# All eight later modulation blocks summed on VectorE, their columns by products with ones, and a new order of attention and routing

## The chip, the cores and the metric

The kernel runs on one core of one Trainium2 chip, in float32 throughout. The metric is the device time of one execution, in microseconds (us). Time before: 1838.23 us, the median of 3 runs (1836.99 to 1841.49).

## What is computed

Two layers of a hybrid diffusion backbone work on 128 prompt tokens and 256 sample tokens of width 1024 (three tiles of 128 tokens). Each layer has two halves:

```
mod = silu(c) @ w_mod + b_mod        # one row for the prompt, one for the sample, 6 x 1024
sh1, sc1, g1, sh2, sc2, g2 = split(mod, 6)
h = rmsnorm(x) * (1 + sc1) + sh1
x = x + g1 * token_mixing(h)         # pooling, windowed attention, latent attention; three gates; one output projection
h = rmsnorm(x) * (1 + sc2) + sh2
x = x + g2 * experts(h)              # router softmax; each of 16 experts takes its best tokens (16 prompt, 32 sample)
```

In blocks of 512 columns the modulation has twelve blocks, and 0 to 3 are sh1 and sc1, 4 and 5 g1, 6 and 7 sh2, 8 and 9 sc2, 10 and 11 g2. sh2 and sc2 are needed as columns (feature on the partition) for the router and the expert input; g1 and g2 as rows.

## The kernel before

**Weights.** SyncE's queue (SP) brings the mixing weights as 57 units of up to 1 MB (`plan_units`, issued in the order `ISSUE`) into a ring of 8 slots. Unit n is issued only when unit n - 8 has been used (`wait_mixing`), and the queue waits in order. The expert weights come as 96 double units of 2 MB a layer (12 for each pair of experts) into 8 double slots; the first three are issued behind the unit `AFTER_ATTENTION`, the others of the first eight when their slots are free, and each further one when the double unit before it in its slot has been used (`load_group`).

**Two ways to a block.** `mod` (line 1509) makes a block on TensorE: 8 products of 32 columns of the conditioning with 512 columns of weights, four of them side by side in the array; ScalarE copies the row out (`mod_row`) and `mod_cols` (line 1521) turns it into columns by four products with the two-column constant `pair`, which VectorE's `mod_cols` (1031) reads. Blocks 0 to 3 and 6 to 9 go this way. `sum_rows` (line 1268) makes a block on VectorE: for each of 8 parts of the weights and each of the two streams one scalar_tensor_tensor adds weights times conditioning to a row that starts as the bias (copied in by POOL's queue); one product with ones then adds over the partitions. Blocks 4, 5, 10 and 11 (`SUMMED`) go this way.

**Order of a layer** (TensorE, from line 1640): blocks 0 to 3 and the turned input; the segments of the input projection; u for the pooling (line 1666); block 6; the turned queries `tq` (1677), keys `tkc` (1682, 1685) and latents `tkv` (1692); block 7; the query projection `wq` (1704); the pooled products (1710); blocks 8 and 9; the key and value projection `wkv` for four tiles (1731), with the turned query heads `tqm` and key heads `tkm` (1725) in between, and the columns of blocks 6 to 9 (`modcol` 1, line 1739) between the second and third key tile. VectorE normalises heads there (`query`, `key`, with POOL's power). Then eight steps m of attention, a pair of heads each: gate product (1565), values of the step before (1605, 1608), branch product (1584), turned probabilities (1593), second gate, turned probabilities, scores of the next step (1550 to 1556), second branch. Gates and branches all use bank 7; ScalarE reads a gate (tanh, 769), VectorE reads a branch (`merge`, 1070). VectorE finds the maxima (`maxima`, 1083 to 1092), ScalarE the exponentials (755 to 762), VectorE divides (`divide`, 1105) and sums blocks 4 and 5 at the end of a step. Then the third gate and branch (8 steps), with blocks 10 and 11 summed.

**Output and routing** (from line 1878). `project_out(n, t, lo, hi)` (1795) makes half n of tile t; VectorE adds it to x (`add_mixed`, 1321 and 1325). Tiles go in the order 1, 2, 0 (the sample is 1 and 2). For each: `turn_x`, ScalarE's `square_x`, `router` (1819), `route` (1827), softmax (`logits`, `affinities`), then for the sample and for the prompt `turn_affinities` (1834), `top` (rounds of MAX8 and MATCH_REPLACE8), `number`, `turn_slots`, `chosen`, and `gather_sample` (1862) and `gather_prompt` (1873), which pick the tokens of four experts out of the scaled x (`normal_x`) by products. `gathered` scales them with sh2 and sc2 on ScalarE (952, 954) and VectorE (1432, 1434) and gives them to the expert products (`project`, 1925). `gate_row` (1849) makes rows of g2, which ScalarE copies out (940).

```
for n, i in enumerate(SUMMED):
    if n >= 2:
        wait_full(pool, l, ("modb", SUMMED[n - 2], 1))
...
if c == 0:
    pe.wait_ge(xcur_ready, (l * NG + gr + 1) * 12)
    for b in range(4):
        begin_pair(b, 1)
```

Of the kernel before, what the change touches and what calls it, by code (L numbers as in the profile page):

```python
# [8 lines left out]
ALU = mybir.AluOpType  # L9
# [97 lines left out]
MODROW = {0: 0, 2: 1, 1: 0, 3: 1, 6: 0, 7: 1}  # L107
# [6 lines left out]
def plan_banks(l):  # L114
# [19 lines left out]
    use(("mod", 6), 1)  # L134
# [6 lines left out]
    use(("mod", 7), 7)  # L141
# [5 lines left out]
    for i in (8, 9):  # L147
        use(("mod", i), (7, 0)[i % 2])
# [6 lines left out]
    for t in range(4):  # L155
        if t == 2:
            use(("modcol", 1), 3)
        for h in range(2):
            use(("tkm", t, h), (3 + 2 * t + h) % 8 if t < 3 else 1 + h)
    for m in range(NM):  # L160
        for j in range(2):
            use(("sa", m, j), 2 * j)
            use(("sb", m, j), 2 * j + 1)
        for j in range(2):
            use(("x", m, j), 4)
            use(("y", m, j), 5)
        use(("o", m), 6)
        for j in (2 * m, 2 * m + 1):
            use(("gate", j // 8, j % 8), 7)
            use(("br", j // 8, j % 8), 7)  # L170
    for i in (4, 5):
# [6 lines left out]
    for name, b in ((("wo", 0, 1), 5), (("wo", 1, 1), 6), (("wo", 0, 2), 7), (("xt", 1, 0), 0), (("xt", 1, 1), 1),  # L178
                    (("wo", 1, 2), 5), (("rpart", 1), 2), (("wo", 0, 0), 6), (("xt", 2, 0), 0), (("xt", 2, 1), 1),
                    (("route", 1), 3), (("rpart", 2), 2), (("wo", 1, 0), 7), (("route", 2), 3), (("xt", 0, 0), 5),  # L180
                    (("afft", 0), 4), (("modb", 10, 0), 6), (("xt", 0, 1), 5), (("modb", 11, 0), 7), (("rpart", 0), 4),
                    (("route", 0), 6), (("slt", 0), 5), (("afft", 1), 6), (("slt", 1), 7)):
# [21 lines left out]
def plan_units():  # L204
# [5 lines left out]
    for i in (6, 7):  # L210
        units += [("mod", i, 0), ("mod", i, 1)]
    units += [("wq", 0, 0), ("wq", 1, 0)]
    for i in (8, 9):
        units += [("mod", i, 0), ("mod", i, 1)]
    units += [("wkv", 0, 0)]
    for b in range(3):
        for h in range(2):
            if b < 2:
                units += [("mod", 4 + b, h)]
            units += [("gate", (b, h), 0), ("gate", (b, h), 1), ("br", (b, h), 0)]  # L220
    for i in (10, 11):
        units += [("mod", i, 0), ("mod", i, 1)]
    for n in range(2):
        units += [("wo", n, 0), ("wo", n, 1)]
# [17 lines left out]
SUMMED = (4, 5, 10, 11)  # L242
# [22 lines left out]
def hybrid_step(nc, a, outs):  # L265
    with ExitStack() as ctx:
# [76 lines left out]
        wsh = view(12800, 2, KB, NE)  # L343
# [50 lines left out]
        bias_in = [sem(f"bias_in{i}") for i in SUMMED]  # L394
# [1685 lines left out]
```

## Time and profile before

| what | value |
|---|---|
| median of 3 runs | 1838.23 us |
| profiled execution, its own time | 1838.3 us |
| its span, first to last instruction | 1836.3 us |
| mean granted TensorE clock | 0.992 of 2.4 GHz |
| TensorE matmuls busy | 1719.0 us, 94% |
| VectorE, ScalarE, GpSimd busy | 568.3, 295.3, 117.4 us |
| HBM traffic over the span | 290 GB/s |

One execution was recorded. Times of rows are us from the first instruction; PE is TensorE, PEld its weight loads, DVE VectorE, ACT ScalarE, POOL GpSimd, SP SyncE; a q behind the name is the engine's own queue. L1565 is line 1565. A float32 product leaves two matmul records. Layer 0 runs to about 925 us, layer 1 follows.

### The profile page before, as it was taken

What the parts mean: (1) busy time and instruction counts of PE and PEld (TensorE: products, weight loads), DVE (VectorE), ACT (ScalarE), POOL (GpSimd) and SP (SyncE); (2) the same over time, 40 slices, a digit from 0 to 9 for tenths busy, and PEclk for the clock granted to TensorE, in tenths of its full rate; (3) what the DMA queues carried; (4) which work ended last, traced back from release to release, by engine and by line L of the source; (5) the groups of instructions that cost most, each with busy time, mean ns of one, the idle gap of its engine ahead of it and who ended that gap; (6) DMA issues with size and microseconds to landing.
All of it is one profiled execution on the core that took longest, in us unless ns stands there. A gap on an engine that the chain in (4) does not pass through costs nothing.

```text
span 1836.3 us, 18935 instructions
## 1 busy us (share of the span) xinstructions
PE 1719.0 (94%) x7216; PEld 803.3 (44%) x7216; DVE 568.3 (31%) x1245; ACT 295.3 (16%) x741; POOL 117.4 (6%) x160
## 2 busy tenths in 40 slices
PE   6998999999899988898899999999999999988987
PEld 3555555554434332242245555555544342323322
DVE  1345544352322111121124355442541221201211
ACT  2234222200200010000022333221021010100100
POOL 1151000000000000000012410000000000000000
PEclk9999999999999999999999999999999999999999
DMA  9453222354799999999993712225547999999997
GB/s 379 186 205 136 85 99 92 142 205 180 284 430 430 431 431 431 431 430 431 428 366 118 281 46 92 92 92 240 206 155 308 430 430 432 430 431 430 430 430 322
DMA packets 49104, 533.79 MB, mean 291 GB/s; under 512 B 5840, under 2 KB 6896, under 8 KB 10384
## 3 DMA queue, kind: packets, MB, share of 16 engines
q1 hardware_dynamic: 45776, 524.39, 68.3%
q0 software_dynamic: 2112, 7.97, 1.1%
q8 instruction: 43, 0.70, 0.1%
q10 hardware_dynamic: 1152, 0.56, 0.1%
q14 instruction: 21, 0.17, 0.0%
HBM read 530.76 MB, written 2.13 MB: 290 GB/s over the span
## 4 chain that ended last, share of the span: by engine, by line
PE 74%; DMA 21%; DVE 2%; ACT 1%; issue 1%; SPq 0%; ACTq 0%; POOL 0%; DVEq 0%; POOLq 0%
PE bank L1925 21%; DMA ring<-in_w_moe 20%; PE bank L1565 13%; PE bank L1584 7%; PE bank L1630 6%; PE bank L1962 5%; PE bank L1795 5%; PE bank L1666 2%; PE bank L1862 2%; PE bank L1731 2%; PE bank L1515 1%; PE bank L1593 1%; PE bank L1704 1%; PE bank L1608 1%; PE bank L1553 1%; PE bank L1556 1%
## 5 line engine op out<-in xcount | busy, mean ns | idle before, releaser
L1565 PE MATMUL bank<-hT,ring 128*128 128x384 f32 x768 | 259.0, 491 | 8.2 <-DVE xn L1070 4.3
L1925 PE MATMUL bank<-M,hT 128*64 128x512 f32 x1024 | 228.8, 595 | 23.6 <-DMA M<-in_w_moe 19.8
L1925 PE MATMUL bank<-ring,hT 128*64 128x512 f32 x1024 | 227.2, 595 | 11.3 <-DMA ring<-in_w_moe 11.3
L1565 PEld LDWEIGHTS bank<-hT,ring 128*128 128x128 f32 x768 | 143.2, 190 | 113.6 <-DVE xn L1070 7.9
L1925 PEld LDWEIGHTS bank<-M,hT 128*64 128x64 f32 x1024 | 72.7, 137 | 170.3 <-issue 139.3
L1925 PEld LDWEIGHTS bank<-ring,hT 128*64 128x64 f32 x1024 | 72.5, 137 | 157.9 <-issue 139.5
L1584 PE MATMUL bank<-M,ring 128*128 128x384 f32 x384 | 134.2, 492 | 4.8 <-ACT M L769 4.8
L1925 PE MATMUL bank<-ring,M 128*64 128x512 f32 x512 | 115.4, 596 | 18.6 <-DMA ring<-in_w_moe 18.6
L1925 PE MATMUL bank<-M 128*64 128x512 f32 x512 | 115.6, 595 | 12.3 <-DMA M<-in_w_moe 12.3
L1630 PE MATMUL bank<-ring,hT 128*128 128x512 f32 (+1 forms) x288 | 119.3, 574 | 1.7 <-DVE hT L1062 1.7
L962 ACT ACTIVATE hT<-bank 128x512 f32<-128x512 f32 x32 | 19.1, 597 | 574.2 <-PE bank L1925 574.2
L1584 PEld LDWEIGHTS bank<-M,ring 128*128 128x128 f32 x384 | 71.0, 190 | 59.8 <-issue 7.9
L1962 PE MATMUL bank<-M 128*128 128x512 f32 x192 | 93.7, 621 | 3.3 <-DVE M L1457 3.3
L1444 DVE SCALAR_TENSOR_TENSOR hT<-hT,bank 128x512 f32<-128x512 f32 x32 | 22.0, 688 | 233.9 <-ACT hT L962 233.9
L1449 DVE SCALAR_TENSOR_TENSOR hT<-hT,bank 128x512 f32<-128x512 f32 x32 | 22.0, 688 | 213.1 <-PE bank L1925 213.1
L1457 DVE TENSOR_TENSOR M<-bank,g2slot 128x512 f32<-128x512 f32 x32 | 22.1, 691 | 210.7 <-PE bank L1925 210.7
L1795 PE MATMUL bank<-ring,xn 128*128 128x512 f32 x192 | 85.4, 596 | 0.0
L1630 PEld LDWEIGHTS bank<-ring,hT 128*128 128x128 f32 x288 | 55.0, 193 | 63.7 <-issue 63.7
L608 POOL TENSOR_TENSOR rstd<-var,mhalf 128x8 f32<-128x8 f32 (+2 forms) x38 | 47.2, 1244 | 470.6 <-DVE var L986 470.5
L1925 PEld LDWEIGHTS bank<-ring,M 128*64 128x64 f32 x512 | 36.9, 137 | 90.3 <-issue 77.8
L1468 DVE TENSOR_TENSOR x<-x,bank 128x512 f32<-128x512 f32 x96 | 66.0, 688 | 30.1 <-PE bank L1962 30.1
L1925 PEld LDWEIGHTS bank<-M 128*64 128x64 f32 x512 | 37.3, 137 | 83.2 <-issue 79.1
(229 smaller groups left out, 1547.4 us busy)
## 6 DMA issues: line engine op xcount, KB each, us to landing
M<-in_w_moe SPq DMA_DIRECT2D x96, 2048.0 KB, 31.6
ring<-in_w_moe SPq DMA_DIRECT2D x96, 2048.0 KB, 30.6
ring<-in_w_mix SPq DMA_DIRECT2D x110, 1024.0 KB, 8.6
ring<-in_w_mix SPq DMA_DIRECT2D x4, 576.0 KB, 4.7
modrow<-in_bias_rows POOLq DMA_DIRECT2D x4, 512.0 KB, 6.7
g2slot<-in_bias_rows POOLq DMA_DIRECT2D x4, 512.0 KB, 7.6
M<-in_counts POOLq DMA_DIRECT2D x2, 768.0 KB, 12.3
out<-x SPq DMA_DIRECT2D x6, 256.0 KB, 2.0
```

What stands on the lines that cost most here:

```text
L608: nc.gpsimd.tensor_tensor(rstd[:, c0:c0 + n], var[:, c0:c0 + n], mhalf[:, 0:n], ALU.pow)\
L1457: V.tensor_tensor(osb[:, n * 512:(n + 1) * 512], bank[b][:, :], g2slot[:, n * 512:(n + 1) * 512], ALU.mult).then_inc(bank_read[b], 1)
L1468: V.tensor_tensor(xs, xs, bank[b][:, :], ALU.add).then_inc(bank_read[b], 1)
L1565: ins = mm(ps[:, 0:TOK], w[:, q, (j % 4) * P:(j % 4 + 1) * P], hT[:, 4 * h + q, :], start=(h == 0 and q == 0), stop=(h == 1 and q == 3))
L1584: ins = mm(ps[:, 0:TOK], w[:, q, (j % 4) * P:(j % 4 + 1) * P], y[:, q, :], start=(q == 0), stop=(q == 3))
L1630: ins = mm(ps[:, 0:n], hT[:, 4 * h + q, t * P:(t + 1) * P], w[:, q, 0:n], start=(h == 0 and q == 0), stop=(h == 1 and q == 3))
L1666: ins = mm(ps[:, 0:TOK], w[:, q, g * P:(g + 1) * P], hT[:, 4 * h + q, :], start=(h == 0 and q == 0), stop=(h == 1 and q == 3))
L1731: ins = mm(ps[:, :], ckvT[:, k, t * P:(t + 1) * P], w[:, k, h * 512:(h + 1) * 512], start=(k == 0), stop=(k == 1))
L1795: ins = mm(ps[:, :], merged[:, kb, t * P:(t + 1) * P], w[:, kb % 4, :], start=(kb == 0), stop=(kb == 7))
L1862: mm(v[:, :, CP:USED], xn[:, t, kb * P:(kb + 1) * P], gsel[:, t, :].rearrange("p (e s) -> p e s", s=SLOTS)[:, :, CP:USED], start=(t == 1), ...
L1925: ins = mm(bank[b][64 * e:64 * e + 64, :], lhs(e, 4 * h + q), w[:, q, :], start=(h == 0 and q == 0), stop=(h == 1 and q == 3))
L1962: mm(bank[b][:, :], selT[:, t * P:(t + 1) * P], osb[:, n * 512:(n + 1) * 512], start=True, stop=True).then_inc(bank_full[b], 1)
```

## The change

The eight blocks 6 to 9, 4, 5, 10 and 11 are now all summed on VectorE. Blocks 6 to 9 are summed in the eight steps of attention without a bias row (the first product is a tensor_scalar; the bias comes in with the columns), half a unit at a time; 4, 5 and 10 in the stage of the third gate; 11 among the additions of the output projection. Their columns are made by `column`: eight products with one column of ones each. The order of units, of banks, of the copies of turned tiles, of attention, of output projection and of routing changes, and the expert products wait for the two halves of their input apart. The core of the diff:

```diff
@@ plan_units
-    for i in (6, 7):
-        units += [("mod", i, 0), ("mod", i, 1)]
-    units += [("wq", 0, 0), ("wq", 1, 0)]
-    for i in (8, 9):
-        units += [("mod", i, 0), ("mod", i, 1)]
-    units += [("wkv", 0, 0)]
...
+    units += [("wq", 0, 0), ("wq", 1, 0), ("wkv", 0, 0)]
+    for b in range(2):
         for h in range(2):
+            i = 6 + 2 * b + h
+            units += [("mod", i, 0), ("gate", (b, h), 0), ("gate", (b, h), 1), ("br", (b, h), 0), ("mod", i, 1)]
+    units += [("gate", (2, 0), 0), ("gate", (2, 0), 1), ("br", (2, 0), 0), ("mod", 4, 0), ("mod", 4, 1), ("mod", 5, 0),
+              ("gate", (2, 1), 0), ("gate", (2, 1), 1), ("br", (2, 1), 0), ("mod", 5, 1)]
+    units += [("mod", 10, 0), ("mod", 10, 1), ("wo", 0, 0), ("wo", 0, 1), ("mod", 11, 0), ("mod", 11, 1), ("wo", 1, 0),
+              ("wo", 1, 1)]
-ISSUE = [1, 2, 3, 4, 5, 6, 0, 7, 9, 10, 11, 8] + list(range(12, NU))
+ISSUE = [1, 2, 3, 4, 5, 6, 0, 7, 9, 10, 11, 8] + list(range(12, NU - 4)) + [NU - 1, NU - 2, NU - 4, NU - 3]
-AFTER_ATTENTION = UNIT_AT["mod", 10, 1]
+AFTER_ATTENTION = UNIT_AT["gate", (2, 1), 1]
-SUMMED = (4, 5, 10, 11)
+SUMMED = (6, 7, 8, 9, 4, 5, 10, 11)
+BIASED = SUMMED[4:]
@@ gpsimd
-                wait_full(pool, l, ("modcol", 1))
-                for n, i in enumerate(SUMMED):
-                    if n >= 2:
-                        wait_full(pool, l, ("modb", SUMMED[n - 2], 1))
+                for n, i in enumerate(BIASED):
+                    wait_full(pool, l, ("col", 8 + n) if n < 2 else ("modb", BIASED[n - 2], 1))
@@ scalar: mod_row of 6, 7, 8, 9 gone; the copies of tq now behind those of tkc and tkv; in the routing
                 turned(1, 0)
-                square_x(2)
                 router_part(1)
                 turned(2, 0)
+                square_x(2)
...
                 normal_x(1)
+                square_x(0)
                 turned(0, 1)
-                square_x(0)
+                normal_x(2)
                 router_part(0)
-                normal_x(2)
-                for i in (11, 10):
...
                 expert_exp(0)
                 normal_x(0)
+                for i in (10, 11):
@@ vector
-                mod_cols(l, 1, 1, 0, KB, 3)
+                def column(i):
+                    ps = wait_full(dve, l, ("col", i))
...
                 for m in range(NM):
                     for j in range(2):
                         divide(l, m, j)
+                    if m in (3, 5, 7):
+                        column(6 + (m - 3) // 2)
                     merge(l, m // 4, 2 * m % 8)
                     for j in range(2):
                         ps = wait_full(dve, l, ("y", m, j))
...
-                    if m + 1 < NM:
-                        maxima(l, m + 1, 0)
+                        if j == 0:
+                            sum_rows(6 + m // 2, m % 2, (0, 1))
                     merge(l, m // 4, 2 * m % 8 + 1)
                     if m + 1 < NM:
-                        maxima(l, m + 1, 1)
-                    sum_rows(4 + m // 4, m // 2 % 2, (2 * (m % 2), 2 * (m % 2) + 1))
+                        for j in range(2):
+                            maxima(l, m + 1, j)
+                    sum_rows(6 + m // 2, m % 2, (2, 3))
                 for j in range(KB):
                     merge(l, 2, j)
-                    if j in (2, 3):
-                        sum_rows(10, j - 2, range(4))
-                    if j in (5, 6):
-                        sum_rows(11, j - 5, range(4))
+                    if j == 1:
+                        column(9)
+                        router_weights()
+                    else:
+                        i, h = {0: (4, 0), 2: (4, 1), 3: (5, 0), 4: (5, 1), 6: (10, 0), 7: (10, 1)}.get(j, (0, 0))
+                        if i:
+                            sum_rows(i, h, range(4))
...
                 add_mixed(0, 1)
+                sum_rows(11, 0, (0, 1))
                 add_mixed(1, 1)
+                sum_rows(11, 0, (2, 3))
+                sum_rows(11, 1, (0,))
                 add_mixed(0, 2)
                 turned(1, 1)
                 x_variance(1)
+                sum_rows(11, 1, (1, 2, 3))
                 add_mixed(1, 2)
+                logits(1)
                 turned(2, 1)
                 x_variance(2)
-                logits(1)
                 affinities(1)
-                add_mixed(0, 0)
                 logits(2)
                 affinities(2)
+                add_mixed(0, 0)
+                top(0, P, TOK, (0, 1, 2, 3))
+                number(P, TOK)
                 turned(0, 0)
-                top(0, P, TOK, (0, 1))
                 add_mixed(1, 0)
-                top(0, P, TOK, (2, 3))
+                slots(0, 1, T)
+                chosen(0, (1, 2))
                 x_variance(0)
-                number(P, TOK)
                 logits(0)
-                slots(0, 1, T)
                 affinities(0)
-                chosen(0, (1, 2))
@@ tensor: mod(l, 6) to mod(l, 9) and their mod_cols gone; tq turned behind tkc and tkv
+                def column(i):
+                    ps = begin(l, ("col", i))
+                    pe.wait_ge(mod_summed, 2 * len(SUMMED) * l + SUM_AT[i, 1])
+                    for s in range(2):
+                        for c in range(4):
+                            ins = mm(ps[:, 2 * c + s:2 * c + s + 1], part_sum(i, s)[:, c * P:(c + 1) * P], ones[:, 0:1],
+                                     start=True, stop=True)
+                    done(l, ("col", i), ins)
...
                         values(l, m - 1)
+                    if m in (3, 5, 7):
+                        column(6 + (m - 3) // 2)
                     branch(l, b, j)
                     turn_probs(l, m, 0)
                     gate(l, b, j + 1)
                     turn_probs(l, m, 1)
+                    branch(l, b, j + 1)
                     if m + 1 < NM:
                         scores(l, m + 1)
-                    branch(l, b, j + 1)
...
                     branch(l, 2, j)
-                    if j < 2:
+                    if j == 0:
+                        column(9)
+                    if j in (3, 6):
...
-                project_out(1, 2, 0, 8)
+                project_out(1, 2, 0, 4)
                 router(1)
-                project_out(0, 0, 0, 4)
-                for h in range(2):
-                    turn_x(2, h)
+                turn_x(2, 0)
+                project_out(1, 2, 4, 8)
                 route(1)
-                project_out(0, 0, 4, 8)
+                project_out(0, 0, 0, 2)
+                turn_x(2, 1)
+                project_out(0, 0, 2, 4)
                 router(2)
+                project_out(0, 0, 4, 6)
+                route(2)
+                project_out(0, 0, 6, 8)
                 project_out(1, 0, 0, 2)
-                route(2)
+                turn_affinities(0, 1, T)
+                project_out(1, 0, 2, 5)
                 turn_x(0, 0)
-                project_out(1, 0, 2, 6)
-                turn_affinities(0, 1, T)
-                project_out(1, 0, 6, 8)
+                project_out(1, 0, 5, 8)
+                turn_slots(0, 1, T)
...
                 route(0)
-                turn_slots(0, 1, T)
+                pe.wait_ge(xn2_ready, 3 * l + 2)
+                gather_sample(0, (0,))
                 turn_affinities(1, 0, 1)
-                pe.wait_ge(xn2_ready, 3 * l + 2)
-                gather_sample(0, (0, 1, 2))
+                gather_sample(0, (1,))
                 turn_slots(1, 0, 1)
-                gather_sample(0, (3,))
+                gather_sample(0, (2, 3))
...
+                        if c == 0 and g == 0:
+                            pe.wait_ge(xcur_back if h else xcur_front, (l * NG + gr + 1) * 6)
+                            for k in (2 * h, 2 * h + 1):
+                                begin_pair(k, 1)
-                        pe.wait_ge(xcur_ready, (l * NG + gr + 1) * 12)
```

## Rows read from the trace of the kernel before

**Rows 1.** The page: busy us, share, instructions; DMA issues, KB each, us to landing.
```profile
PE 1719.0 (94%) x7216; PEld 803.3 (44%) x7216; DVE 568.3 (31%) x1245; ACT 295.3 (16%) x741; POOL 117.4 (6%) x160
...
M<-in_w_moe SPq DMA_DIRECT2D x96, 2048.0 KB, 31.6
```

**Rows 2.** Windows: length, busy PE, PEld, DVE, ACT, POOL, clock, DMA share, GB/s.
```profile
480.00:483.00 3.00, 3.00 (x17) 1.04 (x15) 0.00 (x0) 0.00 (x0) 0.00 (x0) 1.00 0.00 0
...
500.00:540.00 40.00, 40.00 (x175) 13.67 (x176) 8.67 (x14) 2.70 (x5) 0.98 (x2) 1.00 1.01 431
```

**Rows 3.** Chain that ended last, expert stages of both layers: start, us, what.
```profile
479.09 20.82 PE bank L1925 x96
...
910.43 3.67 PE bank L1925 x16
...
1386.62 20.82 PE bank L1925 x96
...
1818.09 3.67 PE bank L1925 x16
```

**Rows 4.** The same chain in layer 0, from the last segment to the first scores.
```profile
112.65 1.90 PE bank L1515 x16
...
115.00 0.49 ACTq L819
...
120.41 11.85 PE bank L1704 x36
...
135.16 3.64 PE bank L1515 x32
...
148.27 0.88 PE bank L1725 x8
...
160.06 3.59 PE bank L1526 x32
163.65 3.34 PE bank L1725 x16
...
167.85 0.49 PE bank L1550 x4
```

**Rows 5.** Timeline of ScalarE before the query projection.
```profile
113.00 0.38 ACT L812 ACTIVATE M<-bank 128x256 f32<-128x256 f32 x1
...
118.00 0.30 ACT L826 ACTIVATE kT<-bank 128x128 f32<-128x128 f32 x1
```

**Rows 6.** Windows around the column products and the first gate, columns as in rows 2.
```profile
164.00:166.00 2.00, 2.00 (x11) 1.91 (x10) 1.79 (x7) 1.13 (x2) 1.11 (x2) 0.50 0.30 74
...
174.00:176.00 2.00, 0.99 (x4) 0.24 (x2) 1.57 (x7) 1.57 (x7) 0.00 (x0) 1.00 0.01 4
```

**Rows 7.** Timeline of VectorE: last key tile, four sums, end of the numbering.
```profile
162.06 0.42 DVE L1246 TENSOR_TENSOR M<-krg,rstd 128x256 f32<-128x256 f32 x1
...
194.14 2.73 DVE L1283 SCALAR_TENSOR_TENSOR modrow<-ring,cs,modrow 128x512 f32<-128x512 f32 x4
...
464.94 0.41 DVE L1379 TENSOR_TENSOR M<-M 16x256 f32<-16x256 f32 x1
```

**Rows 8.** The chain in the attention loop, first wait behind a branch.
```profile
191.01 0.57 DVE xn L1070
```

**Rows 9.** Units of the mixing weights from 340 to 440 us: issue to landing.
```profile
DMA to landing us min/median/max: 4.7/5.0/11.3
```

**Rows 10.** The chain from the first output product to the first gather.
```profile
414.01 20.68 PE bank L1795 x48
...
457.70 0.22 PE bank L1834 x2
...
464.95 0.98 ACT g2slot L940 x2
...
468.94 5.26 PE bank L1862 x24
```

**Rows 11.** Groups of instructions: VectorE's sums, busy us, mean ns, idle before.
```profile
L1283 DVE SCALAR_TENSOR_TENSOR g2slot<-ring,cs,g2slot 128x512 f32<-128x512 f32 x64 | 43.4, 745 | 0.2
```

More of the change, by code:

```diff
@@ L133, in plan_banks @@
         use(("u", g), 1 + g)
-    use(("mod", 6), 1)
     for t in range(T):
@@ L163, in plan_banks @@
             use(("sb", m, j), 2 * j + 1)
+        if m in (3, 5, 7):
+            use(("col", 6 + (m - 3) // 2), 5)
         for j in range(2):
@@ L170, in plan_banks @@
             use(("br", j // 8, j % 8), 7)
+    use(("col", 9), 5)
     for i in (4, 5):
@@ L393, in hybrid_step @@
         layer_in = sem("layer_in")
-        bias_in = [sem(f"bias_in{i}") for i in SUMMED]
+        bias_in = [sem(f"bias_in{i}") for i in BIASED]
         part_summed = sem("part_summed")
@@ L819, in _ @@
                     act.dma_start(dst, src).then_inc(cache_out, 16)
-                for t in range(T):
-                    ps = wait_full(act, l, ("tq", t))
-                    read(l, ("tq", t), F(qT[:, :, t * P:(t + 1) * P], ps[:, :].rearrange("p (b t) -> p b t", t=P), ACT.Copy))
                 for t in range(T):
@@ L838, in _ @@
                 read(l, ("tkv", 1), F(ckvT[:, :, 2 * P:TOK], ps[:, 0:256].rearrange("p (b t) -> p b t", t=P), ACT.Copy))
-                mod_row(l, 7)
+                for t in range(T):
+                    ps = wait_full(act, l, ("tq", t))
+                    read(l, ("tq", t), F(qT[:, :, t * P:(t + 1) * P], ps[:, :].rearrange("p (b t) -> p b t", t=P), ACT.Copy))
                 for t in range(T):
@@ L1045, in mod_cols @@
                 V.tensor_tensor(amp[k][:, lo:hi, :], amp[k][:, lo:hi, :], col(g0), ALU.mult).then_inc(cols_ready, 1)
-                dve.wait_ge(cols_ready, 3 * l + count)
+                dve.wait_ge(cols_ready, 2 * l + count)
             def h_raw(l, kb):
@@ L1670, in _ @@
                     done(l, ("u", g), ins)
-                mod(l, 6)
-                for t in range(T):
-                    ps = begin(l, ("tq", t))
-                    pe.wait_ge(qtok_ready, 3 * l + t + 1)
-                    for b in range(4):
-                        ins = turn_over(ps[:, b * P:(b + 1) * P], qtok[:, t, b * P:(b + 1) * P], ident)
-                    done(l, ("tq", t), ins)
                 for t in range(T):
@@ L1693, in _ @@
                     done(l, ("tkv", k), ins)
-                mod(l, 7)
+                for t in range(T):
+                    ps = begin(l, ("tq", t))
+                    pe.wait_ge(qtok_ready, 3 * l + t + 1)
+                    for b in range(4):
+                        ins = turn_over(ps[:, b * P:(b + 1) * P], qtok[:, t, b * P:(b + 1) * P], ident)
+                    done(l, ("tq", t), ins)
                 for t in range(T):
@@ L1735, in _ @@
                         turn_heads("tqm", t, t)
-                for t in range(2):
-                    turn_heads("tkm", t, 3 + t)
-                begin(l, ("modcol", 1))
-                for i in range(6, 10):
-                    mod_cols(l, 1, i, i - 6, i == 9)
-                for t in (2, 3):
+                for t in range(4):
                     turn_heads("tkm", t, 3 + t)
@@ L1963, in combine @@
                                start=True, stop=True).then_inc(bank_full[b], 1)
-                    if c == 0:
-                        pe.wait_ge(xcur_ready, (l * NG + gr + 1) * 12)
-                        for b in range(4):
-                            begin_pair(b, 1)
                     project_up(0, BANK_G[0])
@@ L2046 @@
     arrays["w_moe"] = expert_units(v)
-    rows = np.zeros((L, len(SUMMED), P, 2, 512), np.float32)
-    for n, i in enumerate(SUMMED):
+    rows = np.zeros((L, len(BIASED), P, 2, 512), np.float32)
+    for n, i in enumerate(BIASED):
         rows[:, n, 0] = v["b_mod"][:, None, i * 512:(i + 1) * 512]
-    arrays["bias_rows"] = rows.reshape(L, len(SUMMED), P, D)
+    arrays["bias_rows"] = rows.reshape(L, len(BIASED), P, D)
     def columns(a, n):
```

101 lines of the change are left out of this document (51 added, 50 removed).

## The prediction

> **What bounds the kernel now.** I read the page first, then the chain of waits over the whole run, then the windows of the expert stage, and last the chain and each engine's timeline in the stages that the change touches. The page shows TensorE busy for 94% of the span [rows 1], but it is an average over two kinds of stage. In the expert stage of each layer the transfers saturate: no byte moves in the 3 us after the first expert product, then 431 GB/s flow without a break [rows 2]. Eight of the 96 double units are in place before that product, and 88 of 2.1 MB follow, 88 x 4.87 = 428 us. So the stage has a fixed length: from its first product to its last wait for weights it takes 910.43 - 479.09 = 431.3 us in layer 0 and 1818.09 - 1386.62 = 431.5 us in layer 1 [rows 3]. What the change does inside it is worth nothing while the stream is full; what counts is how much sooner each layer's first expert product starts. Up to there TensorE is the chain, with short links through ScalarE and VectorE. The two layers repeat each other within 0.1 us a stage, so I work out layer 0 and double it.
>
> The profiled execution took 1838.3 us for a span of 1836.3, and the median of the runs is 1838.23, so the sum needs no shift between them. About 0.3%, 5.5 us, is what a measurement of this kernel can tell from no change.
>
> **Before the query projection.** Removed: blocks 6 and 7, 1.9 us of TensorE each. Block 6's row copy stood on ScalarE ahead of four issues for the caches and the copies of the turned queries, and block 7's products waited for those copies, whose bank they use; hence 112.65 to 120.41 between the last segment product and the query projection [rows 4, 5]. Afterwards ScalarE copies the last u to 113.4, issues the four (0.49 each, 1.95) and makes three pairs of copies at 0.7 each (the 0.27 and the 0.49 of line 826 and 827 overlap). It is done at 117.5. TensorE's own turns need only 3.6 us, to 116.3. The projection starts at 117.6 to 117.7: **-2.7 us**. ScalarE is the limit there, not TensorE, so 1.1 us of the removed products buys nothing.
>
> **Before the key projection.** Blocks 8 and 9 are 3.64 us of pure TensorE between the pooled products and the projection [rows 4]. The bank that the second half of it needs is free at 135.7 - 2.7 = 133.0, before the 134.3 at which it is wanted. The next link, VectorE's sum of squares for tile 0, finds VectorE free 0.3 us before it is asked for. **-3.65 us**, with only that 0.3 us of leeway.
>
> **The last turns.** The columns of blocks 6 to 9 took 16 products, 3.59 us, between the second and the third turned key tile, and the granted clock fell to 1.2 GHz right behind them, so that the 16 records of the last turns took 3.34 us where eight take 0.88 at 2.4 GHz [rows 4, 6]. Afterwards the path is VectorE: its key tile 3 is ready at 162.5 [rows 7], one turn of 0.9, a semaphore, ScalarE's copies to 164.5, then the first scores, against 167.85. **-3.3 us.** These three make -9.65. Bounds: nothing better, since VectorE and ScalarE hold all three; worse by 1.7 if the new idle places between the turns bring a stretch of 3.4 us at 1.2 GHz, as the one just named, over the scores, and by 1.0 if VectorE is late at the key projection.
>
> **The attention loop.** Scores now stand behind the second branch product. Six of the eight steps lose 0.63 to 0.83 us, 4.0 in sum, in which the next gate waits for VectorE to read the bank of the branch just finished [rows 8]; 1.7 us or more of scores now lie between, so this wait goes. ScalarE's read of the gate now has only a turn (0.76) ahead of the branch to hide behind; it takes 0.49 plus 0.1. On VectorE each step gets eight sums instead of four, four at 2.73 us [rows 7]. Those behind the maxima stand ahead of the divisions. Counted from the end of the scores in steps 1 to 3: maxima to 4.9, four sums to 7.6, first division to 8.8, second to 10.1. TensorE wants the first at 9.8 (gate 5.3, values 1.66, branch 2.8), so it is in time by 0.9; the merge then comes 0.2 late for the next gate in steps 1 and 2. The other four sums lie under the second gate, 5.3 us. In steps 4 to 7 the maxima are 1.3 us shorter. VectorE's work is then about 14.5 us of a step of 21.2: covered, by 0.9 us at its tightest. **-3.6 us.** Only the first product of each block and stream becomes cheaper on VectorE; it is off the path.
>
> **The columns.** Added: 4 blocks x 8 products with a full 128x128 load and one moving column, three in the loop, one in the third gate's stage. The nearest row has the same load and two columns: 32 records, 16 products, in 3.59 us, 0.112 a record [rows 4]. 64 records make **+7.2 us**, all on TensorE's path. Bounds: half of that would need a load faster than any row has; a product at 1.2 GHz throughout would double it, +14.4. The Trainium skill (TensorE: Matmul & The Clock Gate, Back-to-back issue gap) has small products down at a floor near 25 ns. By that floor alone the 64 records would cost 1.6 us and the forecast would be 11 us lower; the row speaks for the load as the limit.
>
> **The third gate.** Eight steps of 7.74 us; the turned-over sums for blocks 4 and 5 only move. VectorE has a merge of 1.1 and eight sums of 5.5 in a step, 6.6 under 7.74: covered. **The queues.** The bias copies on POOL wait for the columns that read the same row before them, and are wanted a step of 7.74 us or more later. On SP each unit behind a summed block waits for VectorE; the tightest are the unit for the second output half, issued when the last branch is done and wanted 6.9 us later, and a lone unit lands in 5.0 [rows 9]; and the last block's first unit, behind it, wanted after 8.4 and there at 7.4. The three early expert loads, 14.6 us, now stand ahead of the last branch unit; they go 34 us before it is used.
>
> **The routing.** From the first output product (0) the products themselves are unchanged, 6.9 us a tile and half, 16 of 48 records in 20.68 [rows 10]. Before, the sample's affinities were turned at 43.9, its best found and numbered until 51.3, and the copies of the gate rows (1.0 of the chain) stood ahead of the last router product, since it uses their bank [rows 7, 10]. The first gather began at 54.9. Now the affinities of the sample are turned at 39.6, the four rounds (0.97 each) and the numbering (1.4) end at 45.0, under the last output products. Then the last half tile 47.2, its square and copy on ScalarE, router product 49.7, a scaling of 1.15 and a copy, last router product at 50.6. The gather of the sample need no longer wait for the prompt's affinities and starts there. Those follow at 52.3, turned 52.5, numbered 55.0, slots chosen 55.9; the second half of the gather runs 55.1 to 58.6. The first expert product then comes 2.55 behind the prompt's gather where it was 3.64, for it waits for the front half of the input alone: at 61.2 where it was 65.1. VectorE's 16 sums for block 11 (10.9 us) fall in pauses of 5.4 and more behind the first four additions. **-3.9 us.** Bounds: the gather's 24 records took 5.26 us at the lower clock [rows 10]; at 0.11 a record as elsewhere it would be 1.8 better. If the sums push one addition, it is up to 1.9 worse.
>
> **Sum** for a layer: -9.65 - 3.6 + 7.2 - 3.9 = -9.95; two layers -19.9; 1838.3 - 19.9 = **1818.4 us**.
>
> **Rivals.** (1) *The columns lower the clock.* In both layers the granted clock was 1.2 GHz for 3.4 us just behind the 16 column products [rows 6]. If each of the eight new blocks of them did it, 1.7 us would be lost each, 13.6 in all: 1832. Against it: each block is half as long and stands between dense products, and the clock stayed at 2.4 GHz over the pause before the first branch, where TensorE worked 0.99 of 2 us [rows 6]. The Trainium skill (TensorE: Matmul & The Clock Gate, What's actually happening) sets the clock by how busy the engine was of late; the trace agrees in that it fell behind pauses, but here it fell behind products without a pause. (2) *Preparation is bound by VectorE and ScalarE.* If only the first 2.7 us come through there, the layer gains 3.0: 1832.3. For it: VectorE's leeway of 0.3 us; against it: the links that I followed move with TensorE. (3) *Slower: the sums hold back the divisions.* They stand ahead of the divisions on an in-order queue. If a sum took 1.4 us in place of 0.68, four would take 2.9 more; less 0.9 of leeway that is 2.0 in each of seven steps, 14 a layer, and 1.4 under the second gate eight times, 11. The layer loses 15: 1868. It decides from about 1.15 us a sum. Against it: 128 of them run at 0.745 [rows 11]. (4) *The order does not reach the expert stage:* the weights are not in place when the product wants them. Then the routing's gain goes, 1826; the last of the eight double units should land 58 to 59 after the first output product, wanted one by one from 61.
>
> **Numbers.** Forecast 0.60; clock 0.10; preparation 0.10; fourth 0.08; slower 0.06; the rest, 0.06, on waits I have not seen. Faster by over 0.3%: the forecast, the fourth, and of (1) and (2) three quarters, for they end near the bound: 0.86. Within: 0.08. Slower: 0.06. The range: down by the gather at full clock in both layers (3.6) and by the waits that stay in the loop as I count it (1.8 before the first branch, 0.6 at step 4), half of which may fall away, to 1812; up over the cases (1), (2) and (4), 1833.
>
> **What would show it.** First scores about 9.6 us sooner after the last segment product; loop steps of 21.2 us with no wait of the gate for VectorE; column blocks of 1.8 us at full clock behind them; first expert product 61 us after the first output product; the same 431 us from there. Wrong it is if turned probabilities wait for VectorE in the loop, if column records are far from 0.112, or if the expert stage changes its length.

## The result, and the profile after

The changed kernel takes 1815.88 us, the median of 4 runs (1815.44 to 1816.2), beside 1838.59 for the kernel before: a ratio of 0.9871, 95% interval 0.9858 to 0.9885. That is 22.7 us faster; 19.9 were forecast, and 1818.4 us.

The page of the changed kernel, as [rows 1]. VectorE has 82 us more, TensorE 16.5 less:

```profile
span 1814.3 us, 18937 instructions
PE 1702.5 (94%) x7152; PEld 801.6 (44%) x7152; DVE 650.5 (36%) x1381; ACT 288.4 (16%) x733; POOL 118.5 (7%) x160
```

The chain that ended last in the changed kernel, as [rows 3], [rows 4] and [rows 10] (start, us, what; 1720 is the query projection, 1745 the key and value projection, 1568 the first scores, 1819 the output products, 1957 the expert products):

```profile
90.37 20.65 PE bank L1684 x64
...
115.70 11.85 PE bank L1720 x36
...
130.43 3.45 PE bank L1745 x8
...
155.97 0.49 PE bank L1568 x4
...
337.72 5.36 PE bank L1583 x16
...
405.20 20.68 PE bank L1819 x48
...
466.92 20.82 PE bank L1957 x96
...
898.38 3.67 PE bank L1957 x16
...
1364.25 20.82 PE bank L1957 x96
...
1795.67 3.67 PE bank L1957 x16
```

Read against the chain of before, stage by stage in layer 0 (u is the product of line 1666 before, 1684 after, first at 92.01 before):

| stage, from first product to first product | before | after | difference | forecast |
|---|---|---|---|---|
| start to u | 92.01 | 90.37 | -1.6 | 0 |
| u to query projection | 28.40 | 25.33 | -3.1 | -2.7 |
| to key and value projection | 18.39 | 14.73 | -3.7 | -3.65 |
| to first scores | 29.05 | 25.54 | -3.5 | -3.3 |
| to third gate | 180.46 | 181.75 | +1.3 | +1.8 |
| to output projection | 65.70 | 67.48 | +1.8 | +1.8 |
| to first expert product | 65.08 | 61.72 | -3.4 | -3.9 |
| to last wait for weights | 431.3 | 431.5 | +0.1 | 0 |

In layer 1 the way from the last wait for weights of layer 0 to the first expert product went from 476.19 to 465.87, -10.3; 9.95 were forecast. The expert stage kept its length. So the change did what it says, and nearly each term has its size.

Part of the gain is granted clock, 0.992 in the mean before and 0.998 after. Before, stretches at 1.2 GHz lay at 23 us (6.8 us long), at the column products at 163 and 1071 (3.4 each) and over the gathers at 467 and 1375 (6.8 each), 27.3 us together; after, only the gathers have one, at 461 and 1359 (3.4 each), 6.8 together, leaving out the last 2 us of each kernel. Half of a stretch is the most that it can cost, so at most 10 of the 22 us of span are clock (an estimate from these lengths; less where TensorE waited anyway).

The columns, in groups of instructions of the changed kernel (line, engine, shapes, count, busy, mean ns, idle before), with the sums on VectorE, which [rows 11] answers to:

```profile
L1290 DVE SCALAR_TENSOR_TENSOR g2slot<-ring,cs,g2slot 128x512 f32<-128x512 f32 x120 | 81.9, 746 | 0.8 <-DVE g2slot L1290 0.5
...
L1765 PE MATMUL bank<-const,modrow 128*128 128x1 f32 x64 | 7.8, 251 | 0.0
L1765 PE MATMUL bank<-const,g2slot 128*128 128x1 f32 x64 | 7.6, 248 | 0.0
```

A sum costs the same 0.746 us though nearly twice as many stand on VectorE's queue. One block of column products in the chain of the changed kernel, with its neighbours, and then the windows of the same kernel over it and behind it (columns as in [rows 2]):

```profile
227.54 1.29 PE bank L1626 x12
228.84 1.88 PE bank L1765 x16
230.72 2.69 PE bank L1602 x8
```
```profile
229.00:231.00 2.00, 2.00 (x18) 1.87 (x18) 1.67 (x8) 0.38 (x1) 0.00 (x0) 1.00 0.33 49
231.00:235.00 4.00, 4.00 (x18) 2.58 (x17) 2.45 (x8) 0.60 (x1) 0.00 (x0) 1.00 0.59 244
```

16 records in 1.88 us, 0.117 each, and the clock behind them is full. The block in the stage of the third gate takes 1.68.

### The profile page after: what moved, and what is told of

It is laid out like the page before. It is cut to its first block, busy times and chain, and to the rows that moved or that the text cites. A ratio compares the mean times of both kernels' runs of the same rounds, so it can differ in the third digit from the quotient of the medians.

```text
span 1814.3 us, 18937 instructions
## 1 busy us (share of the span) xinstructions
PE 1702.5 (94%) x7152; PEld 801.6 (44%) x7152; DVE 650.5 (36%) x1381; ACT 288.4 (16%) x733; POOL 118.5 (7%) x160
## 4 chain that ended last, share of the span: by engine, by line
PE 72%; DMA 23%; DVE 3%; ACT 1%; issue 1%; SPq 0%; ACTq 0%; POOL 0%; DVEq 0%; POOLq 0%
PE bank L1957 21%; DMA ring<-in_w_moe 21%; PE bank L1583 12%; PE bank L1602 7%; PE bank L1648 6%; PE bank L1994 5%; PE bank L1819 5%; PE bank L1684 2%; DMA ring<-in_w_mix 2%; PE bank L1886 2%; PE bank L1745 2%; PE bank L1611 1%; PE bank L1720 1%; PE bank L1626 1%; PE bank L1571 1%; PE bank L1574 1%
## 5 line engine op out<-in xcount | busy, mean ns | idle before, releaser
L1290 DVE SCALAR_TENSOR_TENSOR g2slot<-ring,cs,g2slot 128x512 f32<-128x512 f32 x120 | 81.9, 746 | 0.8 <-DVE g2slot L1290 0.5
L1290 DVE SCALAR_TENSOR_TENSOR modrow<-ring,cs,modrow 128x512 f32<-128x512 f32 x120 | 81.5, 745 | 0.3
```

The lines of the kernel that those rows point to most:

```text
L1290: ins = V.scalar_tensor_tensor(acc, w[:, q, :], cs[:, kb, s:s + 1], acc, ALU.mult, ALU.add)
```

## The experiments

All start from the changed kernel. The ratio is to the kernel before on the same chip; that kernel's median moved between 1838.6 and 1841.4 over the sets, so I compare ratios, and stages of profiles. In this section "to output" is from first scores to first output product (249.06 us in the changed kernel, 245.99 before) and "routing" from there to the first expert product (61.9 and 62.0 in the changed kernel, 65.3 and 65.5 before), by the first record of each, which can lie 0.2 us ahead of the start that the chain gives.

| kernel | median us | ratio, 95% interval | span of the profile |
|---|---|---|---|
| scores first | 1824.85 | 0.9910, 0.9885 to 0.9935 | 1824.5 |
| columns twice | 1843.63 | 1.0016, 1.0001 to 1.0031 | 1840.0 |
| sums together | 1832.11 | 0.9954, 0.9939 to 0.9969 | 1830.2 |
| old routing | 1823.19 | 0.9904, 0.9881 to 0.9926 | 1818.9 |
| whole input | 1819.61 | 0.9878, 0.9845 to 0.9910 | 1819.1 |
| half the columns | 1808.44 | 0.9822, 0.9791 to 0.9854 | 1806.3 |
| queries first | 1819.24 | 0.9880, 0.9848 to 0.9913 | 1817.2 |
| gather early | 1813.11 | 0.9850, 0.9817 to 0.9883 | 1810.9 |
| tanh first | 1812.67 | 0.9847, 0.9832 to 0.9862 | 1813.8 |
| three together | 1813.07 | 0.9849, 0.9836 to 0.9863 | 1812.6 |
| changed kernel again | 1816.12 | 0.9870, 0.9855 to 0.9885 | 1813.8 |
| three and filled | 1811.03 | 0.9836, 0.9822 to 0.9849 | 1807.6 |

**Scores first.**
```diff
                     turn_probs(l, m, 1)
-                    branch(l, b, j + 1)
                     if m + 1 < NM:
                         scores(l, m + 1)
+                    branch(l, b, j + 1)
```


> The changed kernel with the scores of the next step put back ahead of the second branch product, on TensorE and in VectorE's order. Theory: the next gate waits again for VectorE to read the branch's bank, 0.6 us and more in six steps of a layer, so 3.5 to 4 us a layer come back: first scores to third gate 185.5 us in place of 181.8, total +7.3 us, 1823. Rival (the loop is bound by VectorE's eight sums, whatever TensorE's order): 1816, or faster.

The edit puts VectorE's first maxima back ahead of the second merge too. To output is 253.3 us in layer 0, +4.3, and 254.5 in layer 1, where a stretch at 1.2 GHz from 1060 lies in it. The chain of this kernel has the wait for VectorE's read of the branch back, as in [rows 8] (start, us, what):

```profile
182.71 0.56 DVE xn L1059
183.31 5.43 PE bank L1584 x16
```

So the order of scores and branch is worth 4.3 us a layer, somewhat more than the 3.6 forecast. The loop is not bound by the sums.

**Columns twice**, and **half the columns.**
```diff
-                    for s in range(2):
+                    for s in (0, 1, 0, 1):
```


> The changed kernel with each of the 32 column products of a layer issued twice, same results. Theory: 64 more records a layer at 0.112 us on TensorE's path, 7.2 us a layer: total +14.4 us, 1830; granted clock still 2.4 GHz in the attention loop. Rival clock: blocks of 3.6 us of such products lower the granted clock to 1.2 GHz behind them, 1.7 us more for each of eight, total +28, 1844. Rival cover (the columns lie in pauses of TensorE): under +5.

```diff
-                    for s in range(2):
-                        for c in range(4):
-                            ins = mm(ps[:, 2 * c + s:2 * c + s + 1], part_sum(i, s)[:, c * P:(c + 1) * P], ones[:, 0:1],
-                                     start=True, stop=True)
+                    for c in range(4):
+                        ins = mm(ps[:, 2 * c:2 * c + 2], part_sum(i, 0)[:, c * P:(c + 1) * P], ones[:, 0:2],
+                                 start=True, stop=True)
```


> The changed kernel with four column products a block in place of eight: the prompt's sums fill both streams' columns, so the sample's shift and scale before the experts are left out. Theory: 16 products less a layer at 0.224 us, 3.6 us a layer, total -7.2 us, 1808.7. Rival cover (they lie in pauses): under -2.

Half the columns took 3.6 us from "to output" in each layer (245.5 against 249.06), as worked out from 0.112 a record, and 8.0 us from the span; the rest of that comes from the routing of layer 0, which had no stretch at 1.2 GHz there and took 60.5 us. Twice the columns cost 25.7 us of span, neither the 14.4 of the theory nor the 28 of the clock rival, but near the second. In six stretches of the loop and the third gate, 27.3 us long together, the granted clock was 1.2 GHz, two of them twice as long as the others. Each began inside one of the eight doubled blocks or up to 0.7 us behind it; at the other two blocks, at 282 and 330 us, the clock stayed. The chain of the kernel with twice the columns over its first block, and then its windows over that block and behind it (columns as in [rows 2]):

```profile
230.27 4.29 PE bank L1765 x32
234.56 5.33 PE bank L1602 x8
239.89 0.86 PE bank L1611 x7
```
```profile
230.00:234.00 4.00, 4.00 (x35) 3.80 (x31) 3.22 (x12) 0.81 (x3) 0.00 (x0) 0.89 0.52 166
234.00:239.00 5.00, 5.00 (x10) 2.92 (x11) 0.17 (x1) 0.00 (x0) 0.00 (x0) 0.50 0.20 82
```

The branch product takes 5.33 us, twice 2.66. TensorE had not paused for 24 us or more before any of the six; it had run products of one column last. 14.4 and half of 27.3, less the 1.6 us a layer by which this run's routing was shorter, is 25. So the rival that I gave 0.10 is a true mechanism. The change met it at none of its eight blocks; the kernel with doubled blocks met it at six of eight.

**Sums together.**
```diff
-                        if j == 0:
-                            sum_rows(6 + m // 2, m % 2, (0, 1))
...
-                    sum_rows(6 + m // 2, m % 2, (2, 3))
+                    sum_rows(6 + m // 2, m % 2, (0, 1, 2, 3))
```


> The changed kernel with all eight sums of an attention step behind the maxima, ahead of the divisions. Theory (VectorE is in time by 0.9 us there): four more sums are 2.7 us, so 1.8 us are lost in steps 1 to 3 before the turned probabilities, and about 0.5 in the others, whose maxima are shorter and whose branch is later: 7 us a layer, total +14, 1830. Rival (leeway is larger than worked out): no change. Rival (VectorE bounds the loop already): no change either, but then the loop's TensorE waits for VectorE in the changed kernel.

To output is 257.1 and 257.2, +8.1 a layer for 7 expected. A stretch of 3.4 us at 1.2 GHz lies in the loop of each layer, at 194 and 1122 us, and up to half of it, 1.7, is the clock's, so the sums themselves cost about 6.4. The chain of this kernel goes through VectorE:

```profile
210.47 5.39 DVE modrow L1290 x8
...
217.96 0.74 DVE M L1094 x2
218.70 0.47 DVE xn L1059
219.22 5.43 PE bank L1581 x16
```

Sums, divisions, merge, gate: the chain goes through the merge behind the second division, which holds the next gate for 0.7 us. Ahead of that the turned probabilities wait for the first division, 1.17 us in step 1 and 1.70 in step 2, and 0.56 for VectorE in step 3. This is the slower rival of the prediction, made to happen: 2.7 us more ahead of the divisions is enough. TensorE lost 1.9 and 2.5 us to both waits in steps 1 and 2, so the leeway there was 0.8 and 0.3 us: it is real and under a microsecond.

**Old routing**, and **whole input.** The first puts back the order from the output projection to the first gather; its core on TensorE:
```diff
-                project_out(0, 0, 4, 6)
+                project_out(1, 0, 0, 2)
                 route(2)
-                project_out(0, 0, 6, 8)
-                project_out(1, 0, 0, 2)
+                turn_x(0, 0)
+                project_out(1, 0, 2, 6)
                 turn_affinities(0, 1, T)
-                project_out(1, 0, 2, 5)
-                turn_x(0, 0)
-                project_out(1, 0, 5, 8)
-                turn_slots(0, 1, T)
+                project_out(1, 0, 6, 8)
```


> The changed kernel with banks, ScalarE's, VectorE's and TensorE's order from the output projection to the first gather as before, block 11 still summed among the additions and the two halves of the expert input still waited for apart. Theory: the new order's 3.4 us a layer go, less 1.1 of them that belong to the half input: first output product to first expert product 64 in place of 61.7, total +4.6 us, 1820.5. Rival (the half input brings it all): no change.

```diff
-                            pe.wait_ge(xcur_back if h else xcur_front, (l * NG + gr + 1) * 6)
...
+                            if h == 0:
+                                pe.wait_ge(xcur_front, (l * NG + gr + 1) * 6)
+                                pe.wait_ge(xcur_back, (l * NG + gr + 1) * 6)
```


> The changed kernel, with the expert products waiting for both halves of their input together, as before the change. Theory: the first expert product comes 1.1 us later behind the prompt's gather, 2.2 us in all, 1818; the later groups gain nothing, since the stream of weights is full there. Rival (the split input helps in each of the four groups of a layer): +8 us.

The routing took 64.4 and 63.4 us with the old order, and the span grew by 4.6, as expected. The first of the two has a stretch of 6.8 us at 1.2 GHz in it, the second one of 3.4, as the changed kernel in its first profile. With the whole input the routing took 61.8 in both layers, in layer 1 without a stretch, where the changed kernel takes 60.3 without one and 61.9 with one (the second run of it shows both, one in each layer). So the split input is worth 1.4 us a layer, the order 1.5 beside a like clock, and a stretch of 6.8 us in place of 3.4 costs 1.0. The whole input's span grew by 4.8, not 2.2, since a stretch at 1.2 GHz fell over its first expert products and another into its second loop.

**Queries first.**
```diff
+                for t in range(T):
+                    ps = wait_full(act, l, ("tq", t))
...
                 for t in range(T):
                     ps = wait_full(act, l, ("tkc", t))
```


> The changed kernel with the turned queries put back ahead of the turned keys and latents, on TensorE and ScalarE. Theory (ScalarE's copies release the query projection): three copies of 0.52 us stand ahead of the keys' again, the projection starts 1.6 us later, 3.1 us in all, 1819. Rival (TensorE's turns are the limit): no change, since they are the same in either order.

From the first u product to the query projection 27.0 and 27.3 us in place of 25.5 and 25.6: ScalarE's three copies (1.57 in its chain) are on the path, and TensorE's turns are not. The span grew by 2.9, near the expected 3.1 by luck: two stretches at 1.2 GHz, at 118 and 156 us, cost 2.4 more in layer 0, and the routing, without a stretch in either layer, took 3.2 less.

**Gather early**, **tanh first**, and **three together.** What the trace of the changed kernel left open: the second half of the gather stood behind the numbering on VectorE and ran at 1.2 GHz. Its chain in layer 0 (1866 turns the slots over, 1886 is the second half of the gather, 1897 the prompt's gather):

```profile
460.87 0.26 PE bank L1866
461.13 3.48 PE bank L1886 x16
464.60 0.85 PE bank L1897 x8
```
```diff
-                gather_sample(0, (0,))
+                gather_sample(0, (0, 1))
                 turn_affinities(1, 0, 1)
-                gather_sample(0, (1,))
-                turn_slots(1, 0, 1)
                 gather_sample(0, (2, 3))
+                turn_slots(1, 0, 1)
```


> The changed kernel with the first gather of the sample in pairs of banks, two ahead of the turned affinities of the prompt and two ahead of its turned slots. Theory: only the prompt's gather is left behind the last chain on VectorE, first output product to first expert product 59 to 59.5 in place of 61.9, and no stretch at 1.2 GHz there; total -5 us, 1811. Rival (the gather delays the turned affinities and so the chain on VectorE): no change.

Routing 59.4 us in both layers, as expected, and faster than the changed kernel by 2.5 a layer; 1.6 of that is the stretch at 1.2 GHz that is no longer in it, and 0.9 the order, against the 60.3 that the changed kernel takes without one. The span fell by 3.4 only: in layer 0 the granted clock fell 0.5 us ahead of the first expert product instead, and everything behind it moved 1.3 later. TensorE had just paused twice, for 0.7 and 0.8 us, and paused again for 0.6 as the clock fell. Windows of the kernel with the gather early, from the last gather to the first expert products (columns as in [rows 2]):

```profile
461.00:464.00 3.00, 1.97 (x17) 1.93 (x17) 1.25 (x6) 1.04 (x4) 0.98 (x2) 1.00 1.00 421
464.00:467.00 3.00, 2.42 (x8) 0.85 (x9) 1.79 (x7) 1.65 (x6) 0.00 (x0) 0.54 0.36 153
```

```diff
-                for j in range(2):
-                    exps(l, 0, j)
+                exps(l, 0, 0)
...
                         gate_tanh(l, (2 * m + j) // 8, (2 * m + j) % 8)
+                        if m == 0 and j == 0:
+                            exps(l, 0, 1)
```


> The changed kernel with ScalarE's tanh of the first gate put between the exponentials of the first two heads, so that the first branch product need not wait for both. Theory: of the 1.8 us that TensorE waits there, 1.2 go in each layer; total -2.4 us, 1813.5. Rival (the second head's exponentials, 1.1 us later, hold back a division that TensorE wants): no change.

To output 248.0 in both layers, -1.1 each. The median is 3.45 us below that of the changed kernel on the same chip, and the loop gives 2.2 of it. The profile is of the slowest of its four runs: its routing, without a stretch at 1.2 GHz in either layer, took 1.6 less in each, and its start of layer 0 took 3 more (below). The third step puts the columns of block 6 at step 4, and the three stand together:

> The changed kernel with the early gather, the early tanh, and the columns of block 6 one step later, at step 4, where the branch product waits 0.56 us for ScalarE anyway. Theory: -2.5 -1.2 -0.6 us a layer, total -8.6, 1807.3; faster than both kernels. A stretch at 1.2 GHz over a first expert product can take 1.7 us of it.

To output 247.6 in both layers, routing 59.4 and 59.4. Moving the columns brought 0.4 a layer, not 0.6. By stages it is 4 us a layer better than the changed kernel, but the median only 3.05 us: a stretch at 1.2 GHz lay over the first expert product in both layers, and one in the start of layer 0 (67.6 us from the first segment product to the first u product, where the changed kernel had 64.4).

> The changed kernel unaltered, on the chip of the two before it. All theories: 1816 within 2 us. Layer 0 up to the first u product, 64.4 us there and 65.4 before the change, should again differ from run to run, for nothing of that stage is changed; then 1 to 1.6 us of the measured gain are the start's and not the change's.

The changed kernel came out at 1816.12 again, with 64.4 us in that stage. The kernels whose profile shows 67.5 to 67.6 there (scores first, tanh first, three together) do exactly the same work up to that point. In them TensorE waited 2.2 us at 40 us for a unit of weights to land, where it waited 0.7 to 0.8 in the two profiles of the changed kernel, and a stretch at 1.2 GHz followed at 43 us. Before the change it was 65.4, without that wait and with 6.8 us at 1.2 GHz at 23 us.

**Three and filled.** The edit is against the kernel with the three:
```diff
                 gather_sample(0, (2, 3))
+                gather_sample(0, (3,))
                 turn_slots(1, 0, 1)
+                wait_read(pe, l, ("modb", 11, 0))
+                mm(bank[BANK_Y][:, :], ident, const[:, 0:512], start=True, stop=True)
                 pe.wait_ge(xn2_ready, 3 * l + 3)
                 gather_prompt(0)
+                mm(bank[BANK_Y][:, :], ident, const[:, 0:512], start=True, stop=True)
```


> The kernel with gather, tanh and columns moved (measured 1813.07 us), with four source products more in TensorE's pauses before the first expert product: the last gather pair repeated, and two products of the identity with constants into a bank that is free; no result is changed. Theory: the granted clock falls to 1.2 GHz over the first expert products there because TensorE pauses before them, and this delays the stream of weights by 1.7 us; filled, the clock stays at 2.4 GHz, the extra work costs 0.3 us, and a layer gains 1.4: total -2.8, 1810.3. Rival (the pauses do not set the clock there): +0.6 us.

The edit repeats one bank of the gather, four source products, so with the two others it adds six. The same two windows in the kernel with the three and the filling:

```profile
461.00:464.00 3.00, 3.00 (x21) 2.13 (x20) 1.67 (x6) 2.13 (x7) 0.98 (x2) 1.00 0.85 360
464.00:467.00 3.00, 3.00 (x15) 1.02 (x16) 0.71 (x3) 0.56 (x2) 0.00 (x0) 1.00 0.04 16
```

TensorE does not pause there any more, and no stretch at 1.2 GHz is left in this profile but one that begins 0.3 us before its end. The routing is 59.9, half a microsecond of it the filling, and the way from the first expert product to the next layer's first segment product is 454.5 us where it was 455.9 in the kernel without the filling. By this profile the filling gains 0.9 us a layer net. But it is the profile of the fastest of five runs, with a mean granted clock of 1.000; the other four had 0.997 to 0.999, so stretches at 1.2 GHz came in them somewhere (without the filling the five had 0.996 to 0.998). Its ratio, 0.9836, is the lowest of the kernels that leave nothing out, but its interval overlaps those of the kernel without the filling, of gather early and of tanh first, so by medians its gain over them is not shown. It does beat both kernels of the case.

## Why the prediction was right

**What bounds the kernel.** The fixed expert stage held: 431.3 before, 431.5 after, and every gain ahead of it came out at the end: 22.4 us at the last wait for weights and 22.0 in the span, for the clock fell in the last 2 us.

**Preparation.** -3.1, -3.7, -3.5 for -2.7, -3.65, -3.3. Queries first shows that ScalarE's copies release the query projection, as the step said. The first of the three is 0.4 larger since ScalarE's queue issued the first of its four transfers beside the last copy, so that they held it for 1.6 us behind that copy and not for 1.95:

```profile
111.36 0.38 ACT L803 ACTIVATE M<-bank 128x256 f32<-128x256 f32 x1
111.36 1.37 ACTq L809 DMA_DIRECT2D out<-M  x3
112.76 0.51 ACTq L809 DMA_DIRECT2D out<-kr  x1
113.31 0.28 ACT L813 ACTIVATE kT<-bank 128x128 f32<-128x128 f32 x1 [1.57 <-issue]
```

The leeway of 0.3 us on VectorE was enough, and rival (2) fell. The clock did not fall in the new pauses between the turns in the profile shown; in five of the other profiles, that of the changed kernel again among them, it did, at 153 to 156 us, and cost 0.7 to 0.9 us.

**Loop.** +1.3 for +1.8: the wait for VectorE's read is gone, which scores first puts at 4.3 a layer and I had at 3.6. Besides the waits the second branch product, with scores behind it, takes 2.66 us in place of 2.78, which I did not count. What is left exposed is what the range of the prediction named, 1.81 us before the first branch and 0.58 at step 4, the same as before the change. The 0.2 that I had before the next gate in steps 1 and 2 came at another place: there the first branch product waits 0.2 us for ScalarE's tanh behind the exponentials. The chain of the changed kernel in step 1:

```profile
185.78 0.39 ACT M L760
186.21 2.85 PE bank L1602 x8
```

**Columns.** +7.2 a layer held, by half of them taken away (3.6). A record took 0.117 us. The floor for small products that the Trainium skill gives (TensorE: Matmul & The Clock Gate, Back-to-back issue gap) does not set the pace of a product with its own 128 columns of load. For such a load the Trainium skill (TensorE: Matmul & The Clock Gate, LDWEIGHTS (loading the stationary operand)) gives its columns divided by 1.2 in nanoseconds, which makes an estimate of 107 ns here, and the measured record is close to that. Rival (1) did not come, but its reading of the kernel before needs a correction: TensorE ran the 16 column products there without a pause, yet it had paused for 1.24 us at 157.8, a little ahead of them, so that row alone does not tell pause from columns. The doubled columns do.

**Routing.** -3.4 for -3.9. The output products ended at 45.6, the last half tile came at 47.8 (forecast 47.2), the last router product at 50.8 (50.6), the numbering ended at 55.5 (55.0), and the second half of the gather began at 55.9 (55.1) and ran at the lower clock, as the sum had assumed; the first expert product then came 2.3 behind it (2.55). So the chain up to that gather is 0.8 longer than the sum had it. Nor is the gain all order: by the two layers of old routing 1.0 of the 3.4 is the clock's, a stretch of 6.8 us at 1.2 GHz before and one of 3.4 now, which the sum did not set apart. Rival (4) fell: no product waited for the first eight double units, and no byte moved from 466 to 470 us.

**What is left.** The forecast gain is 2.8 us short. Layer 0's start is 1.6 of it, in a stage that the change does not touch and that, from the first segment product on, took 64.1 to 67.6 us in the profiles, by when weights landed and where the clock fell: that part is luck. I have one profile of the kernel before, so whether its median holds the same 1.6 stays open. The terms of preparation and loop, less the routing's, make 0.9 us over two layers; 0.4 goes the other way in the last 2 us, and the medians differ by 0.7 more than the profiled spans do.

## What to carry to other kernels

Where a stage has a fixed length by its stream of weights, look for what starts the stream, and count only what comes before; a term read from the chain of waits ahead of it then reaches the end whole. A reduction moved to an idle engine costs nothing until it stands ahead of something short on that engine's queue: place it by the leeway of the next instruction, as four sums before the divisions and four behind the turned probabilities, not all eight together. And keep blocks of products with hardly any columns short, because the clock that falls there is paid by what comes next. Filling pauses ahead of a stream's first product can pay in the same way; one profile shows it here and the medians do not settle it.

## What the runs showed of the hardware

The granted clock fell to 1.2 GHz inside or just behind six of eight blocks of 32 records of one-column products (3.5 to 4.8 us, TensorE without a pause) in one execution, and at none of the 16 blocks of 16 (1.7 to 1.9 us) in the two profiles of the changed kernel. It also fell behind pauses of TensorE, but whether it did so at a given place differed although the place was alike: in the second profile of the changed kernel TensorE paused for 0.9 and 1.6 us ahead of the last gather in both layers, and the gather ran at 2.4 GHz in layer 0 and, for the most part, at 1.2 GHz in layer 1. Windows of that profile over the two gathers:

```profile
462.00:464.00 2.00, 2.00 (x18) 1.97 (x19) 0.60 (x2) 0.00 (x0) 0.98 (x2) 1.00 0.95 410
1359.00:1361.00 2.00, 2.00 (x12) 2.00 (x11) 0.00 (x0) 0.00 (x0) 0.62 (x2) 0.52 1.07 459
```

A gain of 2.5 us ahead of such a place can so come out as 1.2. Differences of 1 to 3 us in this kernel should be read by stages, with the granted clock beside them, and not from the medians.
